# Four loads at the start of a fused decoder layer change queue and order, and the first block's preparation changes order with them

## What is computed

```
def layer(x, ...):
    xn = rmsnorm(x, norm_mix_g[l])                        # x: 256 prompt rows + 32 sample rows
    proj = einsum('bsd,de->bse', xn, w_in[l])             # 1024 -> 2048 columns
    zc, new_conv = conv_mixer(proj[..., :1536], ...)      # gates and a causal conv of width 3
    zp, new_pool = pool_mixer(proj[..., 1536:], ...)      # trailing means of 2, 4, 8, 16 rows
    x = x + einsum('bse,ed->bsd', concat([zc, zp]), w_out[l])
    x = x + moe(rmsnorm(x, norm_ffn_g[l]), ...)           # top 4 of 32 experts, clamped SwiGLU
    return x, new_conv, new_pool
```

## Time and profile before

| | us |
|---|---|
| median of three runs | 1042.14 |
| lowest and highest of them | 1040.13, 1045.3 |
| the profiled execution, own time | 1045.87 |
| its span | 1044.1 |
| TensorE busy | 962.3 (92%) |
| VectorE busy | 297.1 (28%) |
| ScalarE busy | 178.3 (17%) |
| GpSimd busy | 81.5 (8%) |

### The profile page before, as it was taken

How to read it: one execution, slowest core, us unless ns; L and a number is a source line. 1 busy time by engine, 2 the same in 40 slices (tenths; PEclk the granted TensorE clock), 3 DMA queues, 4 the chain that set the end, 5 groups by cost and what they waited for, 6 DMA issues and landing times.

```text
span 1044.1 us, 11538 instructions
## 1 busy us (share of the span) xinstructions
PE 962.3 (92%) x4625; PEld 409.5 (39%) x4625; DVE 297.1 (28%) x523; ACT 178.3 (17%) x375; POOL 81.5 (8%) x75
## 2 busy tenths in 40 slices
PE   8999999999998989989898989989898989989796
PEld 7999433333332323333232323333332323333232
DVE  5897422222211222221221222221211222221124
ACT  5355421101010201001020201001010201001012
POOL 5975002000000000000000000000000000000001
PEclk9999999999999999999999999999999999999988
DMA  9966899999999999999999999999999999999991
GB/s 316 331 269 247 340 427 424 427 427 429 427 428 430 427 429 429 427 429 429 427 429 429 427 429 429 427 429 429 427 429 429 427 429 429 427 427 429 423 414 64
DMA packets 39694, 420.35 MB, mean 403 GB/s; under 512 B 5306, under 2 KB 5854, under 8 KB 13031
## 3 DMA queue, kind: packets, MB, share of 16 engines
q1 hardware_dynamic: 38799, 418.18, 95.3%
q10 hardware_dynamic: 512, 1.63, 0.5%
q0 software_dynamic: 352, 0.13, 0.0%
HBM read 418.62 MB, written 1.49 MB: 402 GB/s over the span
## 4 chain that ended last, share of the span: by engine, by line
DMA 48%; PE 45%; DVE 4%; issue 1%; SPq 1%; POOL 0%; ACT 0%; ACTq 0%; POOLq 0%; DVEq 0%
DMA ring<-in_exp_w 47%; PE psum L879 19%; PE psum L905 15%; PE psum L780 1%; PE psum L715 1%; PE psum L717 1%; PE psum L716 1%; PE psum L828 1%; PE psum L782 1%; PE psum L927 1%; DMA x_acc<-in_x_sample 1%; PE psum L783 1%; DVE x_acc L1414 1%; PE psum L684 1%; DVE ring L1437 1%
## 5 line engine op out<-in xcount | busy, mean ns | idle before, releaser
L879 PE MATMUL psum<-ring,work 128*64 128x512 f32 x2048 | 472.5, 611 | 57.0 <-DMA ring<-in_exp_w 56.6
L879 PEld LDWEIGHTS psum<-ring,work 128*64 128x64 f32 x2048 | 141.9, 140 | 341.5 <-issue 263.4
L905 PE MATMUL psum<-ring,work 128*64 128x512 f32 x1024 | 229.8, 601 | 7.2 <-DMA ring<-in_exp_w 6.6
L905 PEld LDWEIGHTS psum<-ring,work 128*64 128x64 f32 x1024 | 73.8, 138 | 143.9 <-issue 142.9
L1214 ACT ACTIVATE work<-work 128x512 f32<-128x512 f32 x32 | 19.7, 631 | 542.8 <-DVE work L1550 542.8
L1538 DVE TENSOR_TENSOR x_acc<-x_acc,psum 128x512 f32<-128x512 f32 (+1 forms) x90 | 57.5, 678 | 180.6 <-PE psum L928 180.6
L1550 DVE TENSOR_SCALAR work<-psum 128x512 f32<-128x512 f32 x32 | 20.6, 686 | 262.3 <-PE psum L879 262.3
L1568 DVE SCALAR_TENSOR_TENSOR y_low<-psum,gate_of,y_high 128x512 fp32r<-128x512 f32 x32 | 24.0, 751 | 198.9 <-ACT y_high L1222 198.1
L1727 POOL TENSOR_TENSOR x_norm<-x_acc,gain 128x512 f32<-128x512 f32 x2 | 2.5, 1274 | 853.6 <-DVE x_acc L1613 853.5
L1169 ACT ACTIVATE work<-psum,vecs 128x128 f32<-128x128 f32 x128 | 35.2, 382 | 108.9 <-PE psum L828 102.1
L1222 ACT ACTIVATE y_high<-psum,gate_of 128x512 fp32r<-128x512 f32 x32 | 22.0, 687 | 105.7 <-PE psum L905 103.9
(11 more groups left out here) (255 smaller groups left out, 744.3 us busy)
## 6 DMA issues: line engine op xcount, KB each, us to landing
ring<-in_exp_w SPq DMA_DIRECT2D x182, 2048.0 KB, 26.9
ring<-in_exp_w SPq DMA_DIRECT2D x18, 1024.0 KB, 22.8
ring<-in_w_in SPq DMA_DIRECT2D x3, 2048.0 KB, 19.9
ring<-in_w_out SPq DMA_DIRECT2D x1, 4096.0 KB, 12.7
ring<-in_exp_w SPq DMA_DIRECT2D x4, 512.0 KB, 23.7
ring<-in_w_in SPq DMA_DIRECT2D x3, 512.0 KB, 9.5
bias_rows<-in_exp_b SPq DMA_DIRECT2D x12, 64.0 KB, 2.4
out<-x_norm SPq DMA_DIRECT2D x3, 256.0 KB
```

The costliest lines, as they stand in the source:

```text
L879: last = mm(psum[e * SLOTS:(e + 1) * SLOTS, c, :], gathered_t[:, 2 * i + j, e, :], weights[:, c * BANK:(c + 1) * BANK], start=False, stop= ...
L905: last = mm(psum[e * SLOTS:(e + 1) * SLOTS, y_bank + c, :], h_t[:, 4 * i + j, e, :], ring_w2[:, slot, e, j, c * BANK:(c + 1) * BANK], star ...
```

## The change

The samples' load goes to the head of SyncE's queue, ahead of x's tile 0. Block 0's part k = 0 goes from SyncE's queue to ScalarE's, behind x's tile 1. The norm's vector goes from ScalarE's queue to the head of GpSimd's, ahead of the two memsets and the selection that make `ident`. TensorE turns the tiles in the order 2, 0, 1, with the vector and three `keep_awake` matmuls between tiles 0 and 1 (four `keep_awake` matmuls stood there in two pairs before). ScalarE now rounds x's column 0 ahead of block part 0, and column 1 behind it. VectorE does `low_x(0)` ahead of `low_part(0)`.

```
@@ block.sync
+            nc.sync.dma_start(x_acc[0:NS, 2, :], x_sample.rearrange("b t d -> (b t) d")).then_inc(x_landed[2], 16)
             nc.sync.dma_start(x_acc[:, 0, :], x_prompt[0][0:P, :]).then_inc(x_landed[0], 16)
...
-                    nc.sync.dma_start(w_in_sb[:, j, 0:1], w_in_cols[:, 0:1]).then_inc(w_in_begun, 16)
                     nc.sync.dma_start(w_in_sb[:, j, 1:2], w_in_cols[:, 1:2]).then_inc(w_in_next, 16)
@@ block.tensor
-            for t in range(NTILE):
-                if t == 2:
+            for t in (2, 0, 1):
+                if t == 1:
                     pe.wait_ge(vec_begun, 16)
                     nc.tensor.transpose(psum[:, 7, 0:KD], vec_rows[0:KD], ident[0:KD, 0:KD]).then_inc(front_t, 1)
+                    keep_awake(3, ident[:])
                 pe.wait_ge(x_landed[t], 16)
                 for k in range(4):
                     last = turn_x(k, t)
-                    if t == 2:
+                    if t == 1:
                         last.then_inc(x_t_ready, 1)
-                if t < 2:
-                    keep_awake(2, ident[:])
@@ block.scalar
-            nc.scalar.dma_start(vec_rows[G_MIX:G_MIX + KD, :],
-                                norm_mix_g[0].rearrange("(k c) -> k c", c=P)).then_inc(vec_begun, 16)
-            nc.scalar.dma_start(x_acc[0:NS, 2, :], x_sample.rearrange("b t d -> (b t) d")).then_inc(x_landed[2], 16)
+            nc.scalar.dma_start(w_in_sb[:, 0, 0], w_in[0][0:P, IN_COLUMNS[0] * DC:(IN_COLUMNS[0] + 1) * DC]).then_inc(w_in_begun, 16)
...
+            act.wait_ge(front_t_read, 1)
+            high_x(0, 1)
             high_parts(0, 1)
-            act.wait_ge(front_t_read, 1)
-            high_x(0, 2)
+            high_x(1, 2)
             high_parts(1, 2)
@@ block.vector
+            low_x(0)
             low_part(LOW_ON_DVE[0])
-            low_x(0)
             low_x(1)
@@ block.gpsimd
+            nc.gpsimd.dma_start(vec_rows[G_MIX:G_MIX + KD, :],
+                                norm_mix_g[0].rearrange("(k c) -> k c", c=P)).then_inc(vec_begun, 16)
             G.memset(ident[:], 0.0)
```

## The result

| | before | after |
|---|---|---|
| median of 20 runs each | 1042.29 | 1044.82 |
| lowest, highest | 1040.10, 1045.48 | 1041.39, 1047.86 |
| ratio, 95% interval | | 1.0021 (1.0012 to 1.0030) |
| the profiled execution, own time (span) | 1045.87 (1044.1) | 1047.65 (1045.9) |

The changed kernel is 0.21% slower by the ratio, some 2.2 us (the two medians are 2.5 apart). That is within 0.5%, but the interval lies above 1, and the forecast was 0.7 us faster. Times are microseconds throughout. The profiled executions differ by 1.8 us.

The account below looks back on a forecast made before the run. The samples' landing, then TensorE, was taken to bound the start. Part 0 at 9.1 puts the first product at 10.6 and second block at 12.2, a gain of 0.67: 1042.14 - 0.7 = 1041.4 us, range 1038.7 to 1045.5.

Parts of the forecast that it names:

- The samples' wait goes: Start of TensorE's work: the wait for the samples' transfer that ends at 9.57 us disappears.
- TensorE's own queue decides next: TensorE's start: later `ident`, then turns, vector and `keep_awake` sum to 2.1 us; tile 1 turned from 8.1 to 8.4.
- the marker: Start of VectorE's first copy for the mixers (line 1389 before, 1387 now): forecast at 31.6 us instead of 32.29.
- As a first one, 0.77.: GpSimd's queue head: issuing the vector's load ahead of `ident` takes 0.77 us, moving TensorE's first `keep_awake` from 1.73 to 2.50.
- I carry the slow pace to tile 0 and no further.: TensorE's first matmuls: tile 0 still takes the slow 0.80 us; the three `keep_awake` behind the vector take 0.68.
- ScalarE's order costs 0.53: ScalarE's roundings: the first block part now stands between columns 0 and 1, costing the chain 0.53 us.
- Part 0 at 9.1, part 1 by 9.6: Block 0's loads: part 0 lands at 9.1 us (between 8.3 and 9.8), part 1 hardly later than 9.6.
- The vector at 6.8: GpSimd's load of the norm's vector lands at 6.8 us, in time for TensorE at about 7.4.
- The rival on the late vector: TensorE waits for GpSimd's vector load, from a landing at 8.2 us; 2.2 us slower (1044.3), at worst 1047.0; chance 0.20.
- the last item of the forecast's list: Sign of being wrong: a first issue on GpSimd of several us, holding `ident` and all behind it.
- The shift arrives: An earlier TensorE moves the DMA stream and all that follows by the same amount; rival of no arrival, 1042.1, chance 0.05.
- The gain of 0.67: First product and second block: the second block's product starts at 12.2 us instead of 12.89, carried to the end.

Follow-up runs that it names:

- the run with `ident` first: The changed kernel with GpSimd's load of the vector right behind the selection that makes `ident`; 1043.66 us, ratio 1.0014 against before.
- the run with dummy memsets: The changed kernel with the vector's load back on ScalarE's queue, plus nine dummy memsets on GpSimd ahead of `ident`; 1044.17 us, ratio 1.0007 against before.
- the vector at home: The changed kernel with the vector's load on ScalarE's queue behind tile 1, part 0 behind it; 1041.84 us, ratio 0.9991 against before; profiled again, 1042.78.
- part 0 at home: The changed kernel with block 0's part 0 on SyncE's queue behind tile 0, vector still on GpSimd's; 1043.94 us, ratio 1.0011 against before.
- the both-home kernel: The changed kernel with part 0 back on SyncE's queue and the vector back on ScalarE's; 1041.63 us, ratio 0.9989 against before.
- before again: The kernel before, unchanged, profiled a second time; 1042.27 us.

## Why the prediction was wrong, step by step

**The samples' wait goes: right. TensorE's own queue decides next, and its sizes: wrong.** The first column was forecast for 8.45 to 8.75, in the middle 8.60, and came at 11.08: 2.48 later. The terms, forecast beside the profile:

| step | forecast | measured | difference |
|---|---|---|---|
| first matmul | 2.50 | 3.02 | 0.52 |
| to the samples' turns | 3.65 | 3.72 | 0.07 |
| to tile 0's turns | 0.43 | 1.12 | 0.69 |
| tile 0 | 0.80 | 1.05 | 0.25 |
| vector | 0.20 | 0.20 | 0.00 |
| three `keep_awake` | 0.68 | 1.44 | 0.76 |
| to the first column | 0.34 | 0.53 | 0.19 |

The differences sum to 2.48, and the marker was off by nearly as much (34.00 for 31.6). The rows are not prices of causes. Tile 0 was turned when it landed, at 7.8, so the first three rows together, 1.28, are set by that transfer: with `ident` early it was still turned at 7.93 in the run with `ident` first. The forecast's list of what could be late next (TensorE's queue, the vector, block 0's parts) did not hold this wait. The steps that failed are three.

*"As a first one, 0.77."* The term was the issue's duration alone. The issue also starts 0.53 later (1.33) than the memset that stood there before (0.80), and the selection and the first matmul came 1.29 later, which is the term. The duration itself, 0.74 for 0.77, was right. By the run with dummy memsets 1.3 us of late `ident` cost 0.99 to 1.26 at the marker.

*A term that the sum did not have.* It asked when the samples, the vector and the two block parts land, and let tile 0 land as before. Tile 0 was put behind the samples on its own queue, and part 0 was moved beside it to the other. With the first alone it landed at 5.9 to 6.3, hardly later than the 5.5 and 5.9 of before (TensorE idles 0.53 for it with the vector at home); with both it landed at 7.1 to 8.0. The prediction quoted the Trainium skill, page "DMA: Bandwidth & Descriptors", section "Issuing engines are not separate DMA queues", for part 0 and part 1. The traces agree with it (with part 0 on the other queue the changed kernel's tile 0 landed at 7.1 to 8.0, with part 0 at home at 5.9), but it applied to tile 0, not to the pair it was weighed for.

*"I carry the slow pace to tile 0 and no further."* In the profiled execution it went on to 11.2 us, and is 1.2 of the 2.48 (0.25 + 0.76 + 0.19). The 0.20 more on the samples' turns cost nothing, since TensorE then waited for tile 0. The prediction read the granted clock as 1.00 in each of its windows and could not tell why the first records are slow; they ran at the lower clock, ahead of the trace's first clock record. Before, TensorE was at work from 1.73 on, and the fast pace was there at 6.30. In the ten profiles that start at 3.02 to 3.04 the first record of full clock stands at 6.1 to 9.0 in six and at 11.2 to 12.4 in four; in the eight that start at 1.72 or 1.73 it stands at 4.8 to 6.8 in seven and at 10.6 in one. The clock went back to 0.50 behind the idle times of 1.90 and 1.22 (at 9.3 and 9.5), but not after those of 1.62 and 1.05 that the kernel before has ahead of the samples. No order of the kernel sets it for certain: the both-home kernel had it late too, with the early start.

**ScalarE's order costs 0.53: right.** Measured 0.54, as 22.92 less 22.38. Other profiles agree: from the first column to the marker it is 22.36 to 22.40 in the three profiles that have the old order (before, before again, the vector's move alone), and 22.88 to 22.94 in six with the new order, where neither part 0 nor a slow TensorE holds the first product.

**Part 0 at 9.1, part 1 by 9.6: too late, without effect.** They landed at 8.0 and 8.6. Part 0 bound in the kernel with the vector at home, where it came at 8.9, and in the one with the vector ahead of tile 1 (9.4).

**The vector at 6.8: 7.6, in time.** It landed in 4.8 to 6.7 us from its issue in the ten profiles that have it on GpSimd's queue. The rival on the late vector had a time near the measured one (1044.3), but its mechanism did not occur: its row would have been TensorE idle ahead of line 610. There is none in the profiled execution; in two others, `ident` first and the changed kernel's third, TensorE waited 0.3 and 0.2 for the vector, far from the 2.2 of the rival. The Trainium skill's rule, page "SBUF — State Buffer", section "SBUF: two separate sides", that GpSimd's descriptors can be held up by VectorE, does not show in these traces: carried into this kernel it gave a landing at 10.0, and none came later than 8.6. VectorE ran only memsets (0.88 to 1.65) while the load was issued, so the case hardly tries the rule. The other estimate of the prediction, a landing at 2.8, was far too early. What came true is the last item of the forecast's list, a first issue on GpSimd that holds `ident`, though not of several microseconds.

**The shift arrives: right.** The time behind the marker is 1011.8 and 1011.9.

**The gain of 0.67: present, when both causes are gone.** With the vector at home the markers are 31.35 and 31.08, against 32.29 and 31.88 of before. The two means are 0.87 apart, by two profiles each. The kernel with both moves undone lacks both causes too, and its one profile (32.49, slow to 10.6) shows no gain: the clock can take it back. In whole times it can't be told from none: 0.9991, with 1 in the interval. Against the changed kernel it is worth about 0.3% (1.0021 to 0.9991), some 3 us; each was measured against before, not side by side.

**How the 2.2 us divide.** The third profile of the changed kernel has the fast pace, and its marker is 32.02, no different from before's. So late `ident` and late tile 0 together eat the gain of 0.87. In the two others the marker is 1.7 to 2.0 later: tile 0 was turned 0.63 and 0.86 later, and the rest is the slow pace. The mean marker of the three is 33.24, of before's two 32.09: 1.15 later, of the sign of the 2.2 measured and smaller. The rest is not accounted for by so few profiles. Part of the noise is the clock of the later kernel: the two profiled executions first shown have a mean granted clock of 0.980, those with the vector at home 0.985 and 0.981, and their times from marker to end are 1008.9 and 1009.9. Over all timed runs, times fall by about 0.6 us per 0.001 of mean clock. With that taken out by a fit over the runs of all kernels, the changed kernel is 1.6 us slower than before (give or take 0.5), the vector-home one 0.7 faster (0.6), the one with late `ident` alone 0.7 slower, the one with late tile 0 alone 1.1 slower (0.65 each). The two causes, each by itself, thus make 1.4 and 1.8 against vector-home (give or take 0.8 each), and together 2.3 (0.7). That they overlap fits the profiles, where TensorE waits for tile 0 behind a late `ident`, but these intervals do not show it. The kernels that undo one thing of the changed one (the order back, tile 0 first, part 0 home, the `keep_awake` moved) lie between, 0.4 to 0.7 slower than before (0.65 each).

**Open.** What decides when TensorE's clock rises in a given run; whether part 0 makes tile 0 late without a load on GpSimd's queue; how exactly the loss divides between the two causes; and whether the fastest versions (0.9989 to 0.9991) are faster than before.

## What to carry to other kernels

When a load moves, ask of every load that shares the 16 engines with it when it will land, the one that nobody speaks of first: here it was tile 0, ahead of which 0.13 MB went on its own queue and beside which 0.26 MB went on another. A queue is not free because it has no loads: what stands behind the issue decides, and here it was the matrix that TensorE's first matmul needs. A delay at the start that idle time covers in the old order costs in full in the new one, so an edit that is free alone (0.9989) can be what spoils the set (1.0021 with it, 0.9991 without). It was not harmless alone either: it hid a delay behind the samples' earlier landing, which shows only when the landings are read beside the time. And where a clock column reads full but the same instructions take almost twice as long, compare their rows with a stretch where the column reads half.

## What the runs showed of the hardware

- GpSimd's first load starts 0.53 later than a memset in its place (1.33 and 0.80, with 0.82 us idle ahead of it) and takes 0.74: 1.29 for what stands behind it. Issued behind the selection, it had 0.23 idle ahead of it and took 0.75.
- TensorE's warm-up matmuls run at two paces: three `keep_awake` take 0.94 or 1.65 us, four turns 0.60 to 0.66 or 1.06 to 1.12. The slow one is the lower clock: four turns take 1.06 where the granted clock reads 0.50. At a profile's start the column reads 1.00 over equally slow rows, ahead of the trace's first clock record. That record came anywhere from 4.8 to 12.4 us, and at 6.1, 6.2 and 11.2 in three executions of one kernel.
- The same tile-0 load, second on its queue behind the samples, landed 4.7 to 5.1 us from its issue in six profiles and 5.9 to 6.8 in seven, which have part 0 directly behind tile 1 on the other queue and the vector on GpSimd's; 0.13 MB ahead of everything took 2.5 to 3.2 us, where the same load as the third of its queue took 7.66 and 7.3.
